# One gate item moved behind the first half's branch products, and the first half of the merged rows turned by VectorE instead of TensorE

## What is computed

```
h = RMSNorm(x)
[pool | diff | stick | forget | f_logit | g_logit] = h @ w_in         (7428 columns, 4096 of them gates)
o_0 .. o_3 = four causal token mixers of those columns                (256, 512, 256, 256 wide)
merged = sum_n sigmoid(g_logit_n + b_gate_n) * (o_n @ w_branch[rows of n])
x = x + merged @ w_out
x = x + SwiGLU(RMSNorm(x)) @ w_down
```

## Time and profile before

| quantity | value |
| --- | --- |
| median of 3 runs | 846.55 us |
| the profiled execution, its own time | 846.53 us |
| its span (first to last instruction of the trace) | 844.7 us |
| outside the span | 1.8 us |
| TensorE matmuls busy | 840.3 us, 99% |
| TensorE weight loads busy | 697.4 us, 83% |
| VectorE busy | 609.8 us, 72% |
| ScalarE busy | 445.1 us, 53% |
| GpSimd busy | 113.5 us, 13% |
| TensorE clock granted | full in all 40 slices |
| HBM | 197 GB/s over the span |

### The profile page before, as it was taken

The page is one execution under the profiler, slowest core; times in us unless marked ns, Lnnn a source line. Parts: engine busy times, 40 slices in busy tenths (PEclk is TensorE's granted clock), DMA queues, the critical chain, the costliest instruction groups (busy, mean ns, idle before and its releaser), DMA issues.

```text
span 844.7 us, 11101 instructions
## 1 busy us (share of the span) xinstructions
PE 840.3 (99%) x4110; PEld 697.4 (83%) x4110; DVE 609.8 (72%) x894; ACT 445.1 (53%) x650; POOL 113.5 (13%) x89
## 2 busy tenths in 40 slices
PE   9999999999999999999999999999999999999998
PEld 7878888888888888888888888888888888888887
DVE  7896978778677766665479768869697776666643
ACT  6657655754454454444375585557543644444431
POOL 0650201004501000000005402010064000000000
PEclk9999999999999999999999999999999999999999
DMA  9857666586567766666666485765765577766661
GB/s 337 286 170 227 200 211 203 164 271 191 181 200 246 208 211 202 203 221 215 195 182 175 132 242 170 241 208 150 273 188 165 172 236 209 210 196 222 219 192 50
DMA packets 102374, 172.53 MB, mean 204 GB/s; under 512 B 13104, under 2 KB 27952, under 8 KB 102320
## 3 DMA queue, kind: packets, MB, share of 16 engines
q1 hardware_dynamic: 101888, 171.16, 64.7%
q10 hardware_dynamic: 432, 0.66, 0.2%
HBM read 161.82 MB, written 4.19 MB: 197 GB/s over the span
## 4 chain that ended last, share of the span: by engine, by line
PE 93%; DVE 2%; DMA 2%; SPq 1%; ACT 1%; issue 0%; ACTq 0%
PE bulk L1774 29%; PE bulk L1778 29%; PE bulk L1775 29%; DMA raw<-in_w_in_dram 2%; DVE w_lo L1096 2%; PE bankAB L1539 1%; PE bankT L1686 0%; PE bankAB L1675 0%; PE bankAB L1633 0%; ACT w_hi L817 0%; PE bankAB L1548 0%; PE bankO L1644 0%; PE bankO L1704 0%; PE bankO L1698 0%; PE bankO L1697 0%
## 5 line engine op out<-in xcount | busy, mean ns | idle before, releaser
L1096 DVE TENSOR_TENSOR w_lo<-raw,w_hi 128x1024 fp32r<-128x1024 f32 (+1 forms) x288 | 362.2, 1276 | 113.0 <-ACT w_hi L817 110.8
L817 ACT ACTIVATE w_hi<-raw 128x1024 fp32r<-128x1024 f32 (+1 forms) x286 | 294.8, 1046 | 200.5 <-PE bulk L1778 195.2
L1774 PE MATMUL bulk<-w_hi,hT_hi 128*128 128x512 f32 (+1 forms) x880 | 342.9, 390 | 0.2 <-DVE wide L1199 0.2
L1775 PE MATMUL bulk<-w_lo,hT_hi 128*128 128x512 f32 (+1 forms) x880 | 339.2, 386 | 0.0
L1778 PE MATMUL bulk<-w_hi,hT_lo 128*128 128x512 f32 (+1 forms) x880 | 336.2, 386 | 0.0
L1774 PEld LDWEIGHTS bulk<-w_hi,hT_hi 128*128 128x128 f32 x880 | 165.3, 188 | 33.6 <-issue 0.9
L1778 PEld LDWEIGHTS bulk<-w_hi,hT_lo 128*128 128x128 f32 x880 | 165.0, 188 | 33.2
L1775 PEld LDWEIGHTS bulk<-w_lo,hT_hi 128*128 128x128 f32 x880 | 165.4, 188 | 32.0
L1774 PE MATMUL bulk<-w_hi,aT_hi 128*128 128x512 f32 x174 | 67.8, 390 | 0.0
L1778 PE MATMUL bulk<-w_hi,aT_lo 128*128 128x512 f32 x174 | 67.7, 389 | 0.0
L1775 PE MATMUL bulk<-w_lo,aT_hi 128*128 128x512 f32 x174 | 67.7, 389 | 0.0
(11 more groups left out here) (234 smaller groups left out, 712.6 us busy)
## 6 DMA issues: line engine op xcount, KB each, us to landing
raw<-in_w_in_dram SPq DMA_DIRECT2D x110, 512.0 KB, 4.4
raw<-in_w_ffn_up_dram SPq DMA_DIRECT2D x80, 512.0 KB, 4.3
raw<-in_w_ffn_down_dram SPq DMA_DIRECT2D x44, 512.0 KB, 3.7
raw<-in_w_branch_dram SPq DMA_DIRECT2D x20, 512.0 KB, 4.5
raw<-in_w_out_dram SPq DMA_DIRECT2D x16, 512.0 KB, 3.3
wide<-wide SPq DMA_DIRECT2D x160, 32.0 KB, 2.7
bias<-in_b_gate_dram SPq DMA_DIRECT2D x16, 256.0 KB, 4.7
raw<-in_w_ffn_up_dram SPq DMA_DIRECT2D x16, 256.0 KB, 3.1
```

What stands on the lines that cost most here:

```text
L817: act.activation(w_hi[:, g % RING, :, 0:width], raw[:, g % RAW, :, 0:width], ACT.Copy).then_inc(hi_ready, 1)
L1096: vec.tensor_tensor(w_lo[:, g % RING, :, 0:width], raw[:, g % RAW, :, 0:width], w_hi[:, g % RING, :, 0:width].bitcast(F32), ALU.subtract). ...
L1774: pe.matmul(dst, hi, whi, start=(k == ks[0]), stop=False)
L1775: pe.matmul(dst, hi, wlo, start=False, stop=False)
```

## The change

- The eighth gate item (gate 7, the second half of mixer 3's gate) moves behind the four branch items of j = 0. The branch items of j = 0 become units 56 to 60 (before: 60 to 64), gate 7 becomes units 61 to 64 (before: 56 to 59), and units 65 onwards keep their places.
- Mixer 3's sigmoid is taken by halves, two 128x512 instructions for the first half at slot 57 and two for the second at slots 65 and 66, where two of 128x1024 stood at 60 and 61.
- The eight transposes of merged's first half are gone from TensorE. VectorE turns those rows at slot 63 (2 instructions); SyncE's queue writes them out at u = 66 (1 transfer of 512 KB) and reads them back at u = 68 (4 of 128 KB).
- `merged_evac` of j = 0 reads o_d in SBUF. On ScalarE it stays at slot 69; on VectorE it moves from slot 69 to slot 70.

```diff
-ITEMS += [(("gate", g), "w_in", [(OFF["gate"] + g * NC, NC)], KD) for g in range(8)]
+GATES = [(("gate", g), "w_in", [(OFF["gate"] + g * NC, NC)], KD) for g in range(8)]
...
-ITEMS += [(("branch", j, n), "w_branch", [(j * NC, NC)], KB[n]) for j in range(2) for n in range(4)]
+ITEMS += GATES[:7] + [(("branch", 0, n), "w_branch", [(0, NC)], KB[n]) for n in range(4)]
+ITEMS += GATES[7:] + [(("branch", 1, n), "w_branch", [(NC, NC)], KB[n]) for n in range(4)]
...
-    (47, "pv", "fox", 0), (50, "pool_b"), (52, "tr_probs", "fox", 1), (56, "pv", "fox", 1), (68, "tr_merged", 0),
-    (73, "tr_merged", 1)]
+    (47, "pv", "fox", 0), (50, "pool_b"), (52, "tr_probs", "fox", 1), (56, "pv", "fox", 1), (73, "tr_merged", 1)]
...
-TURN_AT = {"dq": 16, "fox": 33, "diff": 48}
+TURN_AT = {"dq": 16, "fox": 33, "diff": 48, "merged": 62}
 SPREAD_AT = {}
-BY_DRAM = ('dq', 'fox', 'diff')
-for _s in ('fox', 'diff'):
+BY_DRAM = ('dq', 'fox', 'diff', 'merged')
+for _s, _between in (("dq", 0), ("fox", 1), ("diff", 1), ("merged", 2)):
     for _a, _way in enumerate(("out", "back")):
-        SPREAD_AT.setdefault(TURN_AT[_s] + AHEAD + _a, []).append((_s, _way))
...
+        SPREAD_AT.setdefault(TURN_AT[_s] + AHEAD + _a * _between, []).append((_s, _way))
...
-    (55, "diff_evac", 0), (56, "pv_evac", "fox", 1), (60, "sigmoid", 3, 0), (61, "sigmoid", 3, 1), (69, "merged_evac", 0),
-    (72, "merged_evac", 1)]
+    (55, "diff_evac", 0), (56, "pv_evac", "fox", 1), (57, "sigmoid_last", 0, 0), (57, "sigmoid_last", 0, 1),
+    (65, "sigmoid_last", 1, 0), (66, "sigmoid_last", 1, 1), (69, "merged_evac", 0), (72, "merged_evac", 1)]
...
-    (55, "diff_evac", 0), (56, "gate", 6), (57, "pv_evac", "fox", 1), (60, "gate", 7), (69, "merged_evac", 0),
-    (71, "merged_evac", 1)]
+    (55, "diff_evac", 0), (56, "gate", 6), (57, "pv_evac", "fox", 1), (63, "turn", "merged"), (65, "gate", 7),
+    (70, "merged_evac", 0), (71, "merged_evac", 1)]
...
             def merged_evac(layer, j):
+                if j == 0:
+                    wait_spread(act, layer, "merged")
+                    for t in range(TT):
+                        lhs_part(layer, ("merged", 0, t), by_quads(hT[0], (0, 4), t), spread_columns("merged", t, (0, 4)))
+                    return
...
             def merged_evac(layer, j):
                 for t in range(TT):
+                    if j == 0:
+                        lhs_rest(layer, ("merged", 0, t), by_quads(hT[1], (0, 4), t), spread_columns("merged", t, (0, 4)),
+                                 by_quads(hT[0], (0, 4), t))
+                        continue
...
+                elif stage == "merged":
+                    turn_blocks(layer, stage, *(merged_ready, (0, 1)), lambda t: merged(t)[:, 0:NC])
```

More of the change, by code:

```diff
@@ L175, in stage_parts @@
     if stage == "tr_merged":
-        return [((stage, args[0], t), ("AB", "TO")[args[0]][t]) for t in range(TT)]
+        return [((stage, args[0], t), "TO"[t]) for t in range(TT)]
     raise ValueError(stage)
@@ L191 @@
 FF_TURN = [_u + 1 for _u in FF_DONE[:-1]] + [FF_DONE[-1] + 4]
-TURN_AT = {"dq": 16, "fox": 33, "diff": 48}
+TURN_AT = {"dq": 16, "fox": 33, "diff": 48, "merged": 62}
 SPREAD_AT = {}
-BY_DRAM = ('dq', 'fox', 'diff')
-for _s in ('fox', 'diff'):
+BY_DRAM = ('dq', 'fox', 'diff', 'merged')
+for _s, _between in (("dq", 0), ("fox", 1), ("diff", 1), ("merged", 2)):
     for _a, _way in enumerate(("out", "back")):
-        SPREAD_AT.setdefault(TURN_AT[_s] + AHEAD + _a, []).append((_s, _way))
-for _s in ('dq',):
-    SPREAD_AT.setdefault(TURN_AT[_s] + AHEAD, []).extend([(_s, "out"), (_s, "back")])
+        SPREAD_AT.setdefault(TURN_AT[_s] + AHEAD + _a * _between, []).append((_s, _way))
 for _p, _u in enumerate(FF_TURN):
@@ L218 @@
     (48, "pool_evac_a"), (48, "sigmoid", 0, 1), (48, "sigmoid", 1, 0), (48, "sigmoid", 1, 1), (48, "pv_evac", "fox", 0),
-    (49, "pool_evac_b"), (52, "probs_evac", "fox", 1), (53, "sigmoid", 2, 1), (53, "sigmoid", 2, 0), (55, "diff_evac", 1),
-    (55, "diff_evac", 0), (56, "pv_evac", "fox", 1), (60, "sigmoid", 3, 0), (61, "sigmoid", 3, 1), (69, "merged_evac", 0),
-    (72, "merged_evac", 1)]
+    (49, "pool_evac_b"), (52, "probs_evac", "fox", 1), (53, "sigmoid", 2, 0), (53, "sigmoid", 2, 1), (55, "diff_evac", 1),
+    (55, "diff_evac", 0), (56, "pv_evac", "fox", 1), (57, "sigmoid_last", 0, 0), (57, "sigmoid_last", 0, 1),
+    (65, "sigmoid_last", 1, 0), (66, "sigmoid_last", 1, 1), (69, "merged_evac", 0), (72, "merged_evac", 1)]
 MIXING_DVE = [
@@ L552, in build @@
         gate_ready = signal("gate_ready", [(g, t) for g in range(8) for t in range(TT)])
-        gate_open = signal("gate_open", [(n, t) for n in range(4) for t in range(TT)])
+        gate_open = signal("gate_open", [(n, t) for n in range(3) for t in range(TT)] + [(3, j, t) for j in range(2) for t in range(TT)])
         gated = signal("gated", [(j, n, t) for j in range(2) for n in range(4) for t in range(TT)])
@@ L1002, in sigmoid, with sigmoid_last @@
                 act.activation(g, g, ACT.Sigmoid).then_inc(gate_open, 1)
+            def sigmoid_last(layer, j, t):
+                act.wait_ge(gate_ready, nth(gate_ready, layer, (6 + j, t)))
+                g = wide[:, t, 3 * D + j * NC:3 * D + (j + 1) * NC]
+                act.activation(g, g, ACT.Sigmoid).then_inc(gate_open, 1)
             def merged_evac(layer, j):
+                if j == 0:
[3 more added lines that the diff above has]
+                    return
                 for t in range(TT):
@@ L1007, in merged_evac @@
                     lhs_part(layer, ("merged", j, t), hT[0][:, 4 * j:4 * j + 4, t * P:(t + 1) * P],
-                             bank[("AB", "TO")[j][t]].rearrange("p (k q) -> p k q", k=4))
+                             bank["TO"[t]].rearrange("p (k q) -> p k q", k=4))
             def ff_gate(layer, p):
@@ L1038, in _ @@
                           diff_evac=diff_evac, gate=nothing, sigmoid=sigmoid, branch=nothing,
-                          merged_evac=merged_evac, ff_gate=ff_gate, ff_up=nothing, turn=nothing, act_turn=nothing, act_evac=act_evac)
+                          merged_evac=merged_evac, ff_gate=ff_gate, ff_up=nothing, sigmoid_last=sigmoid_last, turn=nothing, act_turn=nothing, act_evac=act_evac)
             def first_hi(k):
@@ L1396, in branch @@
                     wait_item(vec, layer, ("branch", j, n), t)
-                    vec.wait_ge(gate_open, nth(gate_open, layer, (n, t)))
+                    vec.wait_ge(gate_open, nth(gate_open, layer, (n, t) if n < 3 else (n, j, t)))
                     g = wide[:, t, n * D + j * NC:n * D + (j + 1) * NC]
@@ L1402, in merged_evac @@
                 for t in range(TT):
+                    if j == 0:
+                        lhs_rest(layer, ("merged", 0, t), by_quads(hT[1], (0, 4), t), spread_columns("merged", t, (0, 4)),
+                                 by_quads(hT[0], (0, 4), t))
+                        continue
                     lhs_rest(layer, ("merged", j, t), hT[1][:, 4 * j:4 * j + 4, t * P:(t + 1) * P],
-                             bank[("AB", "TO")[j][t]].rearrange("p (k q) -> p k q", k=4),
+                             bank["TO"[t]].rearrange("p (k q) -> p k q", k=4),
                              hT[0][:, 4 * j:4 * j + 4, t * P:(t + 1) * P])
@@ L1712, in tr_merged @@
                     pe.wait_ge(merged_ready, nth(merged_ready, layer, (j, t)))
-                    name = ("AB", "TO")[j][t]
+                    name = "TO"[t]
                     take(name, lhs_lo, layer, ("merged", j, t))
```

## The result

The changed kernel takes **852.55 us**, the median of 5 runs, against 846.63 of the kernel before in the same comparison (5 runs): 5.9 us slower, ratio 1.0075 with a 95% interval of 1.0052 to 1.0098. Forecast were 851.3, and 848.6 to 853.4.

A forecast was written before the change was run, and what follows sets the result against it. The prediction took TensorE's own work to bound the kernel (matmuls busy 99% of the span). Removed transposes, -1.78 us, plus waits at unit 70, 2 x 3.24, gave +4.7 on 846.53: 851.2, stated as 851.3, range 848.6 to 853.4.

The forecast's parts named there:

- What is removed: TensorE's transposes of merged's first half, before unit 70: 0.89 us gained per layer, -1.78 us over two layers.
- What is moved at no cost: Gate 7, branch items four units earlier, sigmoid halves and VectorE's turn: inputs in time; tightest, diff, has 3 us left.
- The way by device memory: Merged's first-half rows, written out and read back from 203: there at 215.5, at worst 217.9, before ACT needs them.
- What is late next: At unit 70, VectorE's hT_lo comes after unit 73's split and alternates with GpSimd's additions: TensorE loses 3.24 us per layer.
- The sign to look for: New entry in PE's waits, about 6.5 us in total, released by DVE's hT_lo, 4 times, longest about 2.1.
- Rivals 1 and 2: At unit 70, hT_lo late but not held up: 846.6, chance 0.11; only the first held up: 849.0, chance 0.12.
- rival 3: Rows land late: from 218 on, each us costs a us per layer; three us more gives 857; chance 0.10.
- rival 4: Removed transposes are the whole effect, hT_lo done by 218.58 for unit 70: 844.8 us; chance 0.05.
- rival 1: At unit 70, low part late but not held up by POOL: 0.9 us lost per layer, 846.6 us; chance 0.11.
- the sum: Whole kernel: -1.78 + 2 x 3.24 = +4.7 us on 846.53, giving 851.2; stated as 851.3 us.
- the band of the forecast itself: Whole kernel, main case with both hT_lo held up by POOL's additions: 850.3 to 852.5 us, chance 0.62.

The follow-up runs named there:

- The run that leaves nothing else: Changed kernel with VectorE's low part at slot 69 behind branch (1, 2)'s product, and GpSimd's additions of that branch held until both hT_lo are done: 844.77 us.
- The additions held: Changed kernel with one more GpSimd wait: its additions of branch (1, 2) begin only when both hT_lo of the first half are done; 846.74 us.
- The order alone: Kernel before with only VectorE's low part of the first half moved from slot 69 to 70, still reading PSUM, TensorE still transposing; 849.74 us.

## Why the prediction was right, and where it was not

- **What is removed**, 0.89 us a layer: right. The run that leaves nothing else measured -1.83 for -1.78.
- **What is moved at no cost**: right, 846.47 against 846.42 with that part alone.
- **The way by device memory**: hidden, as said. It was even quicker than its bound: ACT found the rows there at 214.25, where 215.5 had been worked out. That was not because each step was right: the write landed in 2.8 us instead of 5.1 and the four reads were issued in 1.75 us instead of 3.24, while their landing took 5.7 in the median and at most 7.2, beyond the 4.1 and 6.6 of the rows.
- **What is late next**: right, and it decided. hT_lo was said to be done at 220.6 and 222.4 and was done at 220.4 and 222.1; the loss was put at 3.24 us a layer and is 3.17. (The sign to look for, 6.5 us in PE's list of waits, was this loss added up; the list counts only from the end of the matmul before, and shows 5.3.) That hT_lo out of SBUF waits like a split had been taken from another instruction; "The additions held" shows it for hT_lo itself, 677 against 1758 ns, and "The order alone" shows that out of PSUM it does not. The Trainium skill ("SBUF — State Buffer", "Who interferes with whom") states that a VectorE instruction contends with GpSimd's reads when both its inputs are in SBUF, and not with one input there; all three runs agree.
- **Rivals 1 and 2** (not held up; only the first held up) are out by the two durations of 1.75 us; **rival 3** (late rows) by ACT's timeline; **rival 4** by PE's waits. What rival 1 described can be made: with the additions held the time is 846.74, where 846.6 had been given for it.
- **The step that was mis-sized is the sum.** It had no term for TensorE's clock: in each run of the changed kernel the mean grant is below 1, in the profiled one by 3.2 us at half speed after layer 1's wait, which cost 1.6 us. The forecast without it, +4.7, stood against +5.9 measured, and -1.78 + 2 x 3.17 = +4.6 is what the waits alone make. So the median lies just above the band of the forecast itself (850.3 to 852.5). The wider range held it because it had been kept open for late rows, which did not come; for the clock it gave no reason, and to that extent it was luck.

A step that the prediction had not looked at, since it did not matter for the changed kernel, showed in the experiments: the product of branch (1, 2) frees the banks of unit 70. The low part at slot 69 gained nothing because of it.

## What to carry to other kernels

Before moving a preparation behind another engine's work, list everything that the first matmul of the new item waits for, the bank as well as the operands; one slot later cost 3.3 us here with nothing else changed, and such a cost hides easily behind the instruction that the change is about. When an operand's source moves from PSUM to SBUF, look at what GpSimd does in that stretch: here each of four VectorE instructions became 2.6 times as long, and a single wait that held GpSimd back by at most 1.4 us turned a loss of 5.9 us into a gain of 1.8 together with the right order; either of the two alone came out level with the kernel before (846.74 and 846.41). Where TensorE is the bound, a short wait can cost more than it lasts.

## What the runs showed of the hardware

- **Strict turns.** When VectorE's instructions with two inputs in SBUF and GpSimd's additions are both pending, they alternate one by one, also when VectorE has the next one ready at once: 1.75 us each for 0.68 us of work, in all eight cases of two kernels. Over the seven kernels with hT_lo out of SBUF its 28 instructions took either 674 to 685 ns (16, none of which had to let an addition by) or 1744 to 1783 ns (12, each letting one addition by), and nothing between.
- **The clock after a wait.** Single waits of 0.7 to 1.3 us (four kernels, two layers each) left the granted clock at 1.00. Two waits of 1.9 and 0.75 us close together were followed by 3.2 us at 0.50 in one layer and by nothing in the other, though the waits were the same to 0.01 us. Waits of over 5 and of 7.5 us brought it down in both layers. One run of the changed kernel had a mean grant of 0.992 and took 3.9 us more than the others, so the same program may lose more. What decides between the cases stays open.
- **A wait that the profile puts down to nothing.** With the low part at slot 69 the 0.76 us before unit 70 carry the word "issue" in place of a releaser. They were a wait for a PSUM bank, which VectorE's product released 0.1 us before.
